# Four even block rows of the first weights on GpSimd's DMA queue, and an early split of the first MLP's fourth block

## What is computed

```python
def rms_norm(x, g):
    y = xf * lax.rsqrt(jnp.mean(xf * xf, axis=-1, keepdims=True) + EPS)
    return y * g

def modulate(h, shift, scale):
    return h * (1 + scale[:, None, :]) + shift[:, None, :]

mod = silu(c) @ ada_w[l] + ada_b[l]            # D -> 6 D: shifts, scales, gates
h = modulate(rms_norm(x, norm_mix_g[l]), sh_m, sc_m)
u = h @ w_in                                    # D -> 3 D: B, C and x parts
y = (b_g * conv3(c_g * xv)) @ w_out
x = x + g_m * y
h = modulate(rms_norm(x, norm_mlp_g[l]), sh_f, sc_f)
a = relu(h @ w1); x = x + g_f * ((a * a) @ w2)  # D -> 4 D -> D
```

## Time and profile before

| | |
|---|---|
| median of 3 runs | 1159.19 us (1159.13 to 1159.62) |
| profiled execution: time | 1159.78 us |
| profiled execution: span of the core | 1158.0 us |
| TensorE busy with matmuls | 1152.0 us |
| VectorE, ScalarE, GpSimd busy | 867.4, 544.0, 25.2 us |
| moved by DMA | 168.89 MB |

### The profile page before, as it was taken

The page is one execution under the profiler, slowest core; times in us unless marked ns, Lnnn a source line. Parts: engine busy times, 40 slices in busy tenths (PEclk is TensorE's granted clock), DMA queues, the critical chain, the costliest instruction groups (busy, mean ns, idle before and its releaser), DMA issues.

```text
span 1158.0 us, 16336 instructions
## 1 busy us (share of the span) xinstructions
PE 1152.0 (99%) x5839; PEld 968.0 (84%) x5839; DVE 867.4 (75%) x1192; ACT 544.0 (47%) x877; POOL 25.2 (2%) x37
## 2 busy tenths in 40 slices
PE   9999999999999999999999999999999999999999
PEld 6788889988888888888978888888988888888887
DVE  4566888985675675555889988997877778779694
ACT  5322333641341241233677887775675445445521
POOL 2000000000000000200020000000000000000000
PEclk9999999999999999999999999999999999999999
DMA  9977655376666666333245554464133323332311
GB/s 295 290 219 235 190 179 194 119 238 192 198 187 196 197 185 195 94 91 91 74 128 142 131 133 125 110 164 146 39 108 110 109 81 103 108 120 81 109 55 73
DMA packets 207324, 168.89 MB, mean 146 GB/s; under 512 B 5684, under 2 KB 180188, under 8 KB 207260
## 3 DMA queue, kind: packets, MB, share of 16 engines
q1 hardware_dynamic: 207068, 167.92, 49.4%
q10 hardware_dynamic: 160, 0.06, 0.0%
q0 software_dynamic: 32, 0.07, 0.0%
HBM read 153.24 MB, written 2.10 MB: 134 GB/s over the span
## 4 chain that ended last, share of the span: by engine, by line
PE 96%; SPq 3%; DMA 1%; issue 0%; ACT 0%; DVE 0%; ACTq 0%
PE bank L788 25%; PE bank L790 25%; PE bank L789 25%; PE bank L1104 4%; PE bank L1103 4%; PE bank L1102 4%; PE bank L1279 2%; SPq L466 2%; PE bank L1261 2%; PE bank L1251 1%; PE bank L1252 1%; DMA ada_two<-in_ada_w 1%; SPq L485 1%; PE bank L1241 0%; PE bank L970 0%; PE bank L1225 0%
## 5 line engine op out<-in xcount | busy, mean ns | idle before, releaser
L788 PE MATMUL bank<-h_hi,w_hi 128*128 128x512 f32 (+1 forms) x848 | 318.3, 375 | 0.5 <-DVE w_lo L1951 0.5
L790 PE MATMUL bank<-h_hi,w_lo 128*128 128x512 f32 (+1 forms) x848 | 316.7, 373 | 0.0
L789 PE MATMUL bank<-h_lo,w_hi 128*128 128x512 f32 (+1 forms) x848 | 316.6, 373 | 0.0
L1418 ACT ACTIVATE w_hi<-raw 128x1024 fp32r<-128x1024 f32 x149 | 156.5, 1054 | 155.9 <-DMA raw<-in_mlp_w 118.1
L1951 DVE TENSOR_TENSOR w_lo<-raw,w_hi 128x1024 fp32r<-128x1024 f32 x149 | 181.5, 1221 | 35.0 <-ACT w_hi L1418 34.2
L788 PEld LDWEIGHTS bank<-h_hi,w_hi 128*128 128x128 f32 x848 | 159.8, 188 | 28.4 <-issue 0.6
L790 PEld LDWEIGHTS bank<-h_hi,w_lo 128*128 128x128 f32 x848 | 159.7, 188 | 28.3
L789 PEld LDWEIGHTS bank<-h_lo,w_hi 128*128 128x128 f32 x848 | 159.8, 188 | 27.7
L788 PE MATMUL bank<-g_hi,w_hi 128*128 128x512 f32 (+1 forms) x416 | 155.0, 373 | 0.0
L790 PE MATMUL bank<-g_hi,w_lo 128*128 128x512 f32 (+1 forms) x416 | 153.6, 369 | 0.0
L789 PE MATMUL bank<-g_lo,w_hi 128*128 128x512 f32 (+1 forms) x416 | 153.6, 369 | 0.0
(11 more groups left out here) (293 smaller groups left out, 1687.4 us busy)
## 6 DMA issues: line engine op xcount, KB each, us to landing
raw<-in_mlp_w SPq DMA_DIRECT2D x96, 512.0 KB, 4.0
ada_raw<-in_ada_w SPq DMA_DIRECT2D x40, 1024.0 KB, 5.6
w_raw<-in_mlp_w SPq DMA_DIRECT2D x32, 512.0 KB, 3.4
raw<-in_sc_w_in SPq DMA_DIRECT2D x18, 512.0 KB, 4.3
raw<-in_w_kv SPq DMA_DIRECT2D x16, 512.0 KB, 3.9
ada_first<-in_ada_w SPq DMA_DIRECT2D x24, 256.0 KB, 5.6
raw<-in_q_w SPq DMA_DIRECT2D x8, 512.0 KB, 4.8
keys<-qk SPq DMA_DIRECT2D x16, 256.0 KB, 3.1
```

The source lines that it names most:

```text
L788: mm(out[:, cols], weights_hi, hi[:, k, cols], start=(k == 0), stop=False)
L789: mm(out[:, cols], weights_hi, lo[:, k, cols], start=False, stop=False)
L790: return mm(out[:, cols], weights_lo, hi[:, k, cols], start=False, stop=(k == KT - 1))
L1418: go(w_hi[:, jj, :, :], raw[:, jj, :, :], ACT.Copy).then_inc(hi_ok, 1)
```

## The change

The rows `first_raw[:, k]` for k = 0, 2, 4, 6 and the spare pairs for k = 0, 2, 4 are issued by GpSimd, each row behind a wait for the first half of ada unit k. The spare pair of k = 6 and the odd rows stay on SP. In the first MLP, both splits of block 3 stand right behind the norm, ahead of the up loop; the first chunk's up steps are written out on ScalarE and VectorE in place of a loop.

```diff
@@ SP
-                sp.dma_start(first_raw[:, k, :], first_w[:, k, D:D + GROUP * P]).then_inc(
-                    raw_in[k // 2] if k % 2 else first_in[k // 2], 16)
-                if k % 2 == 0:
+                if k % 2:
+                    sp.dma_start(first_raw[:, k, :], first_w[:, k, D:D + GROUP * P]).then_inc(raw_in[k // 2], 16)
+                elif k == KT - 2:
                     c0 = D + GROUP * P
-                    sp.dma_start(spare_raw[:, 0, k:k + 2, :], first_w[:, k:k + 2, c0:c0 + P]).then_inc(
-                        spare_in[k // 2] if k // 2 < KT // 2 - 1 else raw_in[0], 16)
+                    sp.dma_start(spare_raw[:, 0, k:k + 2, :], first_w[:, k:k + 2, c0:c0 + P]).then_inc(raw_in[0], 16)
@@ GpSimd, behind its memsets
+            first_w = sc_w_in[0].rearrange("(k p) n -> p k n", p=P)
+            for k in range(0, KT, 2):
+                pool.wait_ge(ada_in[k % ADA_SLOTS][0], 32 * (k // ADA_SLOTS + 1))
+                pool.dma_start(first_raw[:, k, :], first_w[:, k, D:D + GROUP * P]).then_inc(first_in[k // 2], 16)
+                if k < KT - 2:
+                    c0 = D + GROUP * P
+                    pool.dma_start(spare_raw[:, 0, k:k + 2, :], first_w[:, k:k + 2, c0:c0 + P]).then_inc(
+                        spare_in[k // 2], 16)
@@ ScalarE, first MLP
+                        if isinstance(c, int) and c == 0 and j == 0:
+                            return
                         split(g, jj + 3)
...
-                with act.Fori(0, CH - 1) as c:
+                split(g0, 3)
+                groups(g0, 2, step_up(0), written_out=True)
+                groups(g0 + 2, 2, step_down)
+                with act.Fori(1, CH - 1) as c:
@@ VectorE, first MLP
+            split(MLP0 // GROUP, 3)
             ada_fold(5, NMOD * KT)
...
-                        if jj == 0:
+                        if jj == 0 and not (isinstance(c, int) and c == 0 and j == 0):
                             split(g, 3)
...
-                    groups(4 * c + g0, 2, step_up(c, True))
+                    groups(4 * c + g0, 2, step_up(c, True), written_out=isinstance(c, int))
```

## The result

| | before | changed |
|---|---|---|
| median | 1159.29 us (1158.94 to 1159.62, 6 runs) | 1164.35 us (1163.69 to 1167.27, 6 runs) |
| ratio | | 1.0048 [1.0038, 1.0058] |
| profiled execution: time, span | 1159.78, 1158.0 us | 1164.56, 1162.4 us |
| mean granted clock, by run | 1.000 | 0.999, 0.999, 0.996, 0.999, 0.996, 0.998 |

The change costs 5.1 us; 1160.8 was predicted, and the result is above the range. The two runs with the lowest mean clock are the two slowest, 1167.27 and 1166.36 us.

The account below looks back on a forecast made before the run. TensorE was taken as the bound, busy 1152.0 of 1158.0 us. Opening +2.4, swallowed at 44.05 −0.4, block 3 −0.4 gave +1.6 us on the 1159.19 us median: 1160.8 us, range 1158.7 to 1162.8.

Parts of the forecast that it names:

- the wait at 44.05: First stage, TensorE's wait for the paired unit's second half: it swallows 0.40 us of a late opening.
- Row 0 issued at about 11.25, the spare pair at 12.28, both landing after 5.0 us: First stage, GpSimd's loads: landing at 16.25 and 17.28, they hold ScalarE and make TensorE's opening 2.4 us late.
- a rival with a chance of 0.05: TensorE's clock falls in the longer gap before the opening: up to 5.5 us more, 1166.3 us; chance 0.05.
- The paired unit's landing unchanged: First stage, DMA: the paired unit still lands at 44.05, at worst sharing engines with row 6 for 0.8 us; counted 0.
- Rows 2, 4 and 6 cost nothing: First stage, ScalarE's copies: row 2 may come 1.16 us later free, 3.6 with the chain late; counted at nothing.
- Block 3 −0.4 us: First MLP: TensorE's 0.49 us wait for block 3's low part goes, some 0.1 us returns at block 4.
- Nothing beside: GpSimd's issues ahead of the ada_acc memset and the written-out first chunk were costed at nothing.
- Rival 2: Opening: loads landing later than 5.7 us after issue make it measurably slower, 1162.8 to 1164.7 us; chance 0.15.

Follow-up runs that it names:

- e3: Changed kernel plus seven matmuls on zeros that fill TensorE's gap ahead of the opening; 1163.01 us, ratio 1.0029.
- e1: Kernel before with only the first MLP's edit (block 3's splits moved, first chunk written out); 1158.64 us, ratio 0.9994.
- e4: Changed kernel with row 0 and its spare pair issued by SP at their old place; 1160.54 us, ratio 1.0009.
- e9: Changed kernel once more, unaltered, for a second trace; 1163.93 us.
- e5: Kernel before with the MLP's edit, and row 0 and its spare pair issued by SP behind ada unit 1 instead of ahead; 1162.26 us, ratio 1.0025.
- e10: Kernel before with the MLP's edit, row 0 and its pair issued late by SP, and seven matmuls on zeros filling TensorE's gap; 1161.35 us, ratio 1.0017.
- e7: Changed kernel with ScalarE's x_tile(5) and first_tile(0) put ahead of the copies of row 0; 1161.71 us, ratio 1.0025.
- e2: Kernel before with only the seven loads moved to GpSimd, without the MLP's edit; 1165.59 us, ratio 1.0047.
- e6: Changed kernel with GpSimd issuing row 0 and its pair without the wait for ada unit 0; 1160.47 us, ratio 1.0012.
- e8: Changed kernel with row 0 and its pair back on SP, and rows 2, 4, 6 waiting for one unit sooner; 1159.18 us, ratio 1.0001.

## Why the prediction was wrong

The path of the forecast was right (late spare pair, ScalarE in order, late opening), a second mechanism, the clock, was left out, and the sum was too small by 3.55 us. Step by step:

1. **TensorE is the bound, and a late opening stays in the time but for the wait at 44.05**: right. 0.6 us were swallowed there, 0.4 predicted.
2. **Row 0 issued at about 11.25, the spare pair at 12.28, both landing after 5.0 us**: right in place, short in size. 11.19 and 11.90; row 0 was copied at 16.64, the pair landed after 5.94 us at 17.84. `x_tile(5)` began at 18.19 (17.73 predicted), the opening came at 19.42 (19.0). The term is 2.84 us instead of 2.4. That this looks close is luck: ada unit 0 came 0.53 us sooner (10.71 instead of 11.24), and this start differs from trace to trace (11.37 in e3). Counted from the start of unit 0's strips, the opening came after 5.34 us in the kernel before, 5.34 and 5.32 in e1 and e4, and after 8.71 to 8.73 in the changed kernel, e9 and e3. So the change makes it 3.4 us late, and the term was short by 1.0 us. GpSimd's issue started 0.48 us behind the strips that wait for the same semaphore, where the forecast had 0.01, and the spare pair took 5.94 us instead of 5.0; the issue of row 0, 0.71 us instead of 1.03, and ScalarE's steps gave some back.
3. **The sum has no term for the clock: this is the step that failed.** The forecast put the longer gap at 2.8 us and left the work behind it at full speed; the clock's fall was a rival with a chance of 0.05, on the ground that no row showed the lower level. No row showed a gap of more than 0.5 us in this stage either, so the rows said nothing for or against it. The runs showed it in both traces of the changed kernel, 1.45 and 1.5 us each, and 4.1 us in e5's trace; e3 and e10, with the gap filled, never lost the clock. Filling the gap took 1.3 us off the changed kernel's median. That doesn't make up the miss: at full clock e3 still stands 3.4 us above its kernel before, where 1.6 were forecast, for the short term of step 2 and the end of step 7. The rival's own bound of 5.5 us held in every trace (4.1 at most). The Trainium skill ("TensorE: Matmul & The Clock Gate", section Part 1) says that the gate lets half the pulses through after idleness; the trace agrees, with a granted clock of 0.50 behind 3.74 us of it, though not every run of e5 and e7 lost the clock.
4. **The paired unit's landing unchanged**: not contradicted; TensorE came too late to wait for it.
5. **Rows 2, 4 and 6 cost nothing**: right in the changed kernel's trace, and only because its opening was late. With row 0 in time they make TensorE wait 1.1 us (e4). The working let row 2 come 1.16 us late against a copy at 23.54; gated on unit 2 it was copied at 26.90.
6. **Block 3 −0.4 us**: 0.49 gained in the trace, and none of it given back at block 4, which was to be 0.1 us late.
7. **Nothing beside**: wrong by about 0.7 us. The end of the program got longer by 0.33 us within the span and 0.38 outside it (below). Its cause is open.

Of the 5.1 us, then, in rounded shares of the profiled execution: +2.8 opening, +1.45 clock, −0.6 and −0.5 given back, +0.7 at the end, +0.9 in the attention, which the repeat (e9) doesn't have; their sum, 4.8 us, is that execution's own difference. The median of the runs differs by 5.06 us, with two runs of six at a mean clock of 0.996. Rival 2, a landing slower than 5.7 us, was half right: the spare pair took 5.94.

No kernel here beats the one before by more than can be measured; e1 is the best, and takes the half of the change that has no load in it.

## What to carry to other kernels

A load's wait is placed by when its data is wanted minus the whole time to landing, here some 6 us at full DMA engines, and not by when the engine's other inputs arrive; what is queued in order behind its consumer counts as late with it. When an edit lengthens a gap of the bounding engine to several microseconds, the granted clock belongs in the sum as a term of its own, even where the windows of before show full clock everywhere, for they may hold no such gap. A term costed at nothing under the cover of another delay should be priced once without that cover, or repairing the first delay uncovers it. And a delay read off two traces should be counted from the event that starts the chain in each: here the start of the chain alone moved by 0.5 us from trace to trace and made a short estimate look close.

## What the runs showed of the hardware

- The lower clock's length varies much from run to run behind nearly the same gap: some 3 us at 0.50 to 0.68 in the changed kernel's trace behind 3.74 us, about 9 us in e2's and e5's behind 3.77 and 3.11 us, and a mean clock of 1.000 in three of e5's nine runs and four of e7's seven (of these runs no trace was kept, so their gaps aren't known). TensorE was busy throughout the slow stretches of the traces. What decides on it stays open.
- Loads from GpSimd's queue took much the same at both sizes: 5.4 us for 256 KB and 5.9 us for 128 KB in the median, while the engines moved 290 to 335 GB/s in all.
- With all seven loads on GpSimd (the changed kernel, e2, e3, e6, e7, e9), 3.20 to 3.29 us pass from the last matmul's start to the end of the span and 2.0 to 2.2 us lie outside it; with none or five there (before, e1, e4, e5, e8, e10) it is 2.85 to 2.91 and 1.7 to 1.9. The output's last DMA is issued in both 0.76 to 0.77 us behind that matmul. No run tells why. In these runs the number of loads and whether row 0's two are among them change together.
- At the start of the program the column of the granted clock and the durations disagree. The same matmul on zeros (first the kernel before at its start, then e3 in the filled gap; ns, shortest, median and longest):

```profile
L901 PE MATMUL bank<-c_wide x20: 379/634/796, 1.2 to 8.4; 128*128 128x256 f32 x20
L1038 PE MATMUL bank<-c_wide x14: 379/379/382, 16.2 to 19.0; 128*128 128x256 f32 x14
```

The granted clock reads 1.00 in the windows of both, yet half of those at the start take 1.7 times as long or more, as at the lower level. So the forecast's "no row shows the lower level" rests on a column that doesn't tell it at the start; the durations of before did show TensorE slow there.
